# Gated recurrences: the output gate's weight tile streamed among the first scores of its own pair of heads

## What is computed

```
q, zf, zb, i, g = split(h @ w_in, 5)          # each 256 x 1024, 8 heads of 128
logf = logaddexp(log_lb, log_1m_lb + log_sigmoid(z)); k = 1 - exp(logf)   # for zf and zb
o = scan(q * 128**-0.5, k_f, logf_f, v=i) + reversed scan(q, k_b, logf_b, i)
o = rms_norm(o, g_norm) * silu(g);  y = o @ w_out
```

## Time and profile before

| | |
|---|---|
| median of 3 runs | 2884.41 us |
| the profiled execution | 2884.56 us, of which its span is 2882.7 |
| mean granted TensorE clock | 0.992 |
| busy, PE / PE weight loads / DVE / ACT / POOL | 97% / 90% / 68% / 50% / 3% |
| chain that ended last | PE 88%, DVE 6%, ACT 3% |
| this mixer, first instance | 226.31 (half 8 of pair 0) to 398.13 us (last tile) |
| this mixer, second instance | 1877.06 to 2050.07 us |

### The profile page before, as it was taken

How to read it: one execution, slowest core, us unless ns; L and a number is a source line. 1 busy time by engine, 2 the same in 40 slices (tenths; PEclk the granted TensorE clock), 3 DMA queues, 4 the chain that set the end, 5 groups by cost and what they waited for, 6 DMA issues and landing times.

```text
span 2882.7 us, 48145 instructions
## 1 busy us (share of the span) xinstructions
PE 2800.3 (97%) x20356; PEld 2594.5 (90%) x20356; DVE 1951.7 (68%) x2547; ACT 1439.9 (50%) x1970; POOL 94.5 (3%) x147
## 2 busy tenths in 40 slices
PE   9999989999998999999999999999899999999998
PEld 8999879999996999998889999998799989988997
DVE  5757876565665656556665565588755788767877
ACT  5445554444456444445644444456444644455543
POOL 0000000000012000001100000000000100000000
PEclk9999999999999999999999999999999999999999
DMA  7654436676552665663346556443465456554563
GB/s 245 205 162 147 124 120 195 190 211 184 160 171 64 202 183 175 195 187 95 108 139 185 175 191 188 154 147 111 139 194 187 151 180 207 179 161 139 175 214 102
DMA packets 406282, 478.46 MB, mean 166 GB/s; under 512 B 16634, under 2 KB 332820, under 8 KB 406068
## 3 DMA queue, kind: packets, MB, share of 16 engines
q1 hardware_dynamic: 404244, 469.07, 51.7%
q0 software_dynamic: 1632, 6.25, 0.8%
q10 hardware_dynamic: 192, 0.08, 0.0%
HBM read 474.29 MB, written 1.05 MB: 165 GB/s over the span
## 4 chain that ended last, share of the span: by engine, by line
PE 88%; DVE 6%; ACT 3%; issue 2%; POOL 0%; DMA 0%; ACTq 0%; POOLq 0%; DVEq 0%
PE Wk L710 18%; PE Wk L712 18%; PE Wk L711 18%; PE Y L710 10%; PE Y L711 10%; PE Y L712 9%; DVE w_lo L2000 2%; DVE work L2300 1%; PE Y L819 1%; PE Wk L1090 1%; ACT w_hi L1425 1%; PE Y L1000 1%; PE Y L1074 0%; PE Wk L1074 0%; PE Y L1103 0%
## 5 line engine op out<-in xcount | busy, mean ns | idle before, releaser
L2000 DVE TENSOR_TENSOR w_lo<-ring,w_hi 128x1024 fp32r<-128x1024 f32 (+2 forms) x910 | 1068.1, 1199 | 560.9 <-ACT w_hi L1425 516.9
L710 PE MATMUL Wk<-xT_hi,w_hi 128*128 128x256 f32 x4320 | 1230.0, 285 | 6.9 <-DVE w_lo L2000 3.5
L712 PE MATMUL Wk<-xT_hi,w_lo 128*128 128x256 f32 x4320 | 1222.3, 283 | 0.0
L711 PE MATMUL Wk<-xT_lo,w_hi 128*128 128x256 f32 x4320 | 1222.2, 283 | 0.0
L1425 ACT ACTIVATE w_hi<-ring 128x1024 fp32r<-128x1024 f32 (+1 forms) x894 | 906.9, 1039 | 596.9 <-PE Wk L712 420.0
L710 PEld LDWEIGHTS Wk<-xT_hi,w_hi 128*128 128x128 f32 x4320 | 828.3, 192 | 18.1 <-issue 7.0
L711 PEld LDWEIGHTS Wk<-xT_lo,w_hi 128*128 128x128 f32 x4320 | 828.5, 192 | 4.7 <-issue 1.0
L712 PEld LDWEIGHTS Wk<-xT_hi,w_lo 128*128 128x128 f32 x4320 | 828.4, 192 | 0.0
L710 PE MATMUL Y<-w_hi,hid_hi 128*128 128x512 f32 x936 | 369.1, 394 | 5.0 <-issue 3.0
L711 PE MATMUL Y<-w_lo,hid_hi 128*128 128x512 f32 x936 | 366.5, 392 | 0.0
L712 PE MATMUL Y<-w_hi,hid_lo 128*128 128x512 f32 x936 | 365.4, 390 | 0.0
(11 more groups left out here) (308 smaller groups left out, 2658.3 us busy)
## 6 DMA issues: line engine op xcount, KB each, us to landing
ring<-in_ffn_w_gu SPq DMA_DIRECT2D x352, 512.0 KB, 4.5
ring<-in_ffn_w_down SPq DMA_DIRECT2D x224, 512.0 KB, 4.2
ring<-in_ffn_w_up SPq DMA_DIRECT2D x96, 512.0 KB, 6.0
ring<-in_hg_w_in SPq DMA_DIRECT2D x80, 512.0 KB, 3.7
ring<-in_na_w_in SPq DMA_DIRECT2D x24, 512.0 KB, 4.5
ring<-in_hg_w_out SPq DMA_DIRECT2D x16, 512.0 KB, 3.3
ring<-in_lru_w_in SPq DMA_DIRECT2D x16, 512.0 KB, 4.1
ring<-in_kv_w SPq DMA_DIRECT2D x16, 512.0 KB, 5.1
```

What stands on the lines that cost most here:

```text
L710: pe.matmul(o, l_hi, r_hi, start=first, stop=False)
L711: pe.matmul(o, l_hi, r_lo, start=False, stop=False)
L712: return pe.matmul(o, l_lo, r_hi, start=False, stop=last)
L2000: ins = dve.tensor_tensor(l, r, h.bitcast(F32), ALU.subtract)
```

## The change

With `HG_LEAD = 8` the stream of halves is shifted by two against the scores. Before pair 0's score 0 only halves 4 to 7 are made. Behind scores 0 and 1 of pair p stand halves 8 and 9 (tile g) of that pair; behind scores 2 to 8 stand halves 0 to 6 of pair p+1, and then half 7. In pair 3, halves 8 and 9 stand behind scores 1 and 2, and the four `pair_out` behind scores 3 to 6; `output` and `squares_summed` of pair 2 come ahead of them. ScalarE and VectorE are shifted to match: splitting runs two units less far ahead of the scores; `save_g` moves from slot 0 to 2 (3 in the last pair), `g_sigmoid` from slot 1 to 3 (4), `gate_of` from 2 to 4 (6); `save_z` from slot 4 to 6, the sigmoid of z from slots 4, 5, 6 to 6, 7, 7; `one_minus` from 7 to 8; `save_q`, `bounded` and `start_queries` from slots 6 and 7 to 8. The clamp of the gate becomes a function of its own, `clamp_g`. Ahead of pair 0 VectorE no longer stands any split between `save_z` and `both_ways`, and `splits(base + 6)` is gone.

```diff
--- before.py
+++ after.py
@@ -29,7 +29,8 @@
 S_BANKS = (0, 1, 6)
 A_BANKS = (0, 1, 6, 7)
 MS_BANKS = (4, 4, 0, 2)
-HALVES_LAST = (0, 0, 1, 1, 2, 2, 3, 4, 5)
+HALVES_LAST = (0, 0, 1, 1, 2, 3, 3, 4, 5)
+HG_LEAD = 8
 LEVELS = 8
 SCORES = LEVELS + 1
 HALVES_AHEAD = 4
@@ -1036,22 +1037,28 @@
                     y_half(a, n, first=j == 0)
 
                 enter(s, (bank(1), bank(2)))
-                for i in range(4, 10):
+                for i in range(4, HG_LEAD):
                     half_product(0, i)
                 for p_ in range(HG_PAIRS):
                     last = p_ == HG_PAIRS - 1
                     for i in range(SCORES):
                         score(p_, i)
+                        if last and i == 0:
+                            output(p_ - 1)
+                        if last and i == 1:
+                            squares_summed(p_ - 1)
                         if not last:
-                            half_product(p_ + 1, i)
-                        if p_ and i == 2 - 2 * last:
+                            half_product(*divmod(10 * p_ + HG_LEAD + i, 10))
+                        elif 1 <= i < 3:
+                            half_product(p_, HG_LEAD + i - 1)
+                        if p_ and not last and i == 2:
                             output(p_ - 1)
-                        if p_ and i == 4 - 3 * last:
+                        if p_ and not last and i == 4:
                             squares_summed(p_ - 1)
-                        if last and i in (0, 2, 4, 6):
-                            pair_out(i // 2 % 2, i // 4)
+                        if last and 3 <= i < 7:
+                            pair_out(i % 2 == 0, (i - 3) // 2)
                     if not last:
-                        half_product(p_ + 1, 9)
+                        half_product(p_ + 1, HG_LEAD - 1)
                 output(HG_PAIRS - 1)
                 pair_out(2, 0)
                 squares_summed(HG_PAIRS - 1)
@@ -1654,7 +1661,6 @@
                 one_minus(Q0)
                 splits(base[s] + 5)
                 save_values(0)
-                splits(base[s] + 6)
                 for p_ in range(HG_PAIRS):
                     Q, last = Q0 + p_, p_ == HG_PAIRS - 1
                     for i in range(SCORES):
@@ -1664,20 +1670,22 @@
                             facing_keys(p_, i + 1)
                         if i in (0, LEVELS - 1, LEVELS):
                             keep(p_, i)
-                        if i == 1:
+                        if i == 3 + last:
                             g_sigmoid(Q)
                         if not last:
-                            ahead(HALVES_AHEAD + 10 * (p_ + 1) + i, s)
+                            ahead(HALVES_AHEAD + 10 * p_ + HG_LEAD + i, s)
                         if p_ and i == 3 and not last:
                             squares_of(p_ - 1)
                         if p_ and i == 5 - 3 * last:
                             roots(p_ - 1)
                         if not last:
-                            if 4 <= i < 7:
-                                z_sigmoid(Q + 1, i - 4)
+                            if i == 6:
+                                z_sigmoid(Q + 1, 0)
                             elif i == 7:
+                                z_sigmoid(Q + 1, 1)
+                                z_sigmoid(Q + 1, 2)
+                            elif i == LEVELS:
                                 one_minus(Q + 1)
-                            elif i == LEVELS:
                                 save_values(p_ + 1)
                         else:
                             ahead(HALVES_AHEAD + 38 + HALVES_LAST[i], s)
@@ -2244,6 +2252,10 @@
                     dve.tensor_tensor(hg_g[:, Q % 2, :].rearrange("p (a t) -> p a t", t=T),
                                       bank(4).rearrange("p (a t) -> p a t", t=T), r_wide(2), ALU.mult)\
                         .then_inc(g_saved, 1)
+
+                def clamp_g(p_):
+
+                    Q = Q0 + p_
                     dve.wait_ge(g_saved, Q + 1)
                     if Q:
                         dve.wait_ge(sg_ready, Q)
@@ -2334,26 +2346,29 @@
                 dve.wait_ge(r_ready, norms_before(s) + 1)
                 splits(base[s] + 3)
                 save_z(0)
-                splits(base[s] + 4)
+                bounded(0)
                 save_q(0)
-                bounded(0)
-                splits(base[s] + 5)
                 start_queries(0)
                 both_ways(0)
                 multiply_blocks(Q0, LEVELS - 1)
-                splits(base[s] + 6)
+                splits(base[s] + 5)
                 for p_ in range(HG_PAIRS):
                     Q, last = Q0 + p_, p_ == HG_PAIRS - 1
                     for i in range(SCORES):
+                        if last and i == 3:
+                            save_g(p_)
                         if 1 <= i < LEVELS:
                             double(p_, i)
                             if i < LEVELS - 1:
                                 keep(p_, i)
                             if 2 <= i < LEVELS - 1:
                                 multiply_blocks(Q, LEVELS - i)
-                        if i == 0:
+                        if i == 2 and not last:
                             save_g(p_)
-                        elif i == 2:
+                            clamp_g(p_)
+                        if i == 3 and last:
+                            clamp_g(p_)
+                        if i == 4 + 2 * last:
                             gate_of(p_)
                         if p_ == HG_PAIRS - 2 and i == 5:
                             split_pair(0)
@@ -2362,15 +2377,13 @@
                         if p_ and i == 6 - 3 * last:
                             normed(p_ - 1)
                         if not last:
-                            ahead(HALVES_AHEAD + 10 * (p_ + 1) + i, s)
-                            if i == 4:
+                            ahead(HALVES_AHEAD + 10 * p_ + HG_LEAD + i, s)
+                            if i == 6:
                                 save_z(p_ + 1)
-                            elif i == 6:
+                            elif i == LEVELS:
                                 save_q(p_ + 1)
-                            elif i == 7:
                                 bounded(p_ + 1)
                                 start_queries(p_ + 1)
-                            elif i == LEVELS:
                                 both_ways(p_ + 1)
                                 multiply_blocks(Q + 1, LEVELS - 1)
                         else:
```

## The result

The changed kernel takes 2901.63 us (median of three, 2901.40 to 2902.04) against 2884.41: a ratio of 1.0058 (95% interval 1.0043 to 1.0072), **17 us slower**. The direction was forecast; the size was not, for 2901.6 lies above the range's end of 2899. The profiled execution took 2902.04, of which its span is 2900.2.

What follows compares the result with a forecast made beforehand. TensorE, 88% of the chain that ended last, was taken as the bound. Instances of +2.5 and +1.4 make +3.9 at full clock; +3.2 slow outputs and +2.1 new gaps give +9.2 on 2884.4: 2893.6 us, range 2875 to 2899.

Steps and rivals of the forecast that it cites:

- start, each instance: Ahead of pair 0: halves 8 and 9 leave this stretch, so score 0 is issued 6.00 us earlier, at 226.31.
- chain from double 6 to score 0: Turn between pairs: VectorE and ScalarE steps in queue order sum to 17.7 us against TensorE's 14.2.
- pair 0: First pair's window: 42.5 us against 39.87, +2.6; in the second instance +1.5 against 40.93.
- pair 1: Second pair's window: 44.1 us against 40.48, +3.6, from waits before score 8 and the next score 0.
- pair 2: Third pair's window: about 44.8 us, +4.2, as it also splits the result of pair 0 in slot 5.
- last pair: Pair 3, from its score 0 to the last tile: 42.9 us at full clock against 44.84, -1.9.
- clock, whole kernel: TensorE clock falls: 3.2 us for slow outputs plus 2.1 for new gaps, on top of the full-clock sum.
- two slow outputs: The output of pair 3 stays as slow as before, +1.6 us in each instance, 3.2 in all.
- After a fall 0.8 of the 1.6 is hidden in pairs 1 and 2: Where VectorE waits for score 3, 0.8 us of a clock fall's 1.6 would not show; in pair 3 none is hidden.
- The first, that the clock holds: Rival: no new gap lowers the clock, +3.9 us, 2888.3; chance 0.20.
- The second (faster): Rival: pair turns are covered, decided at slot 8's low split (1.6 us); -7.9 per instance, 2869 to 2872; chance 0.18.
- The third, 2904: Rival, slower than 2899: all six gaps and the wait before pair_out drop the clock, up to +20 us; chance 0.10.

Runs made afterwards that it cites:

- the filled kernel: The changed kernel with idle products on TensorE ahead of each score 0 of pairs 1 to 3, the first pair_out and each score 8: 2887.40 us, ratio 1.0014.
- The best order found with the shift: The changed kernel with slot 8's low split, save_z, normed, one last-pair split and the gate's sigmoid in all pairs reordered: 2853.94 us, ratio 0.9901.
- the one order tried without it that gained anything: The kernel before with the gate's sigmoid behind the high split in slot 1 and normed in slot 8 ahead of the low split: 2874.20 us, ratio 0.9967.

## Why the prediction was right, and where it was wrong

| term | forecast | after, both instances | at full clock |
|---|---|---|---|
| start, each instance | -6.0 | score 0 at 226.67 (226.3 forecast), no wait | |
| chain from double 6 to score 0 | 17.7 | 17.81 (pair 1) | |
| pair 0 | 42.5 | 42.42, 42.42 | 42.43 |
| pair 1 | 44.1 | 46.59, 45.64 | 44.12 |
| pair 2 | 44.8 | 46.26, 46.25 | 44.77 |
| last pair | 42.9, or 44.5 with a slow output | 46.80, 46.98 | 42.65 |
| clock, whole kernel | 5.3 | some 15 | 0 |

**Right: the start, the chain, every pair's length, and the sign.** Score 0 of pair 0 came without a wait; the waits before score 8 were 1.36 to 2.32 (1.5 to 2.2 forecast) and before score 0 3.24, on the lines that were named. The step that carried most was to add up one chain over two queues in program order. The experiments bear out its links one by one: an early sigmoid changes nothing as long as the low split stands ahead of `bounded`; with that split moved, the wait falls from 3.24 to 0.33.

**Wrong: the clock term.** The step that failed reads "I take one per instance at about 1.05, 2.1 in all", with 3.2 for two slow outputs. From the table, pairs 1 and 2 and the last pair together are 2.47 + 1.49 + 4.15 and 1.52 + 1.48 + 4.33 over their full-clock length: 15.4 where 5.3 was forecast. The kernel at full clock closes the sum from the other side: 17.2 less 4.2 leaves 13, and of the difference to 15.4 about 1 is what came back elsewhere; the interval of the filled kernel reaches 3 to either side. Three things were mis-sized.

- How many falls. "Since the nearest pair of rows fell once in two" was the reason, and one in three turns was taken. Of the five gaps of 3.2 before a score 0, four brought the clock down. At the sixth turn, the last of the first instance, the wait of 2.32 before score 8 had brought it down first. The two halves behind that took 7.5 instead of 6.0, which left 1.76 of the wait before score 0. By then the clock was back (granted 1.00 from 357.00 to 363.00), score 0 ran in its usual 0.69, and the clock fell once more during the output behind it (0.50 from 363.75 to 366.75):

```profile
361.94 0.69 PE L1001 MATMUL Wk<-work 128*64 128x64 f32 x16 [1.76 <-DVE work L2294]
362.55 2.90 PE L1014 MATMUL Y<-work 128*128 128x256 f32 x8
```

  The prediction put the falls before score 8 and before `pair_out` at nothing. The gap of 1.87 before `pair_out` brought it down in both instances: from there to score 4 it was 4.51 and 4.18, where 2.93 is usual. The rows on which the choice rested had a gap of 1.86. The prediction itself says that the new gap is longer, and priced it all the same at a third of its turns.
- What a fall costs. "After a fall 0.8 of the 1.6 is hidden in pairs 1 and 2, where VectorE waits for score 3" runs the wrong way round: where VectorE waits for the score, whatever delays TensorE delays the whole chain. In pair 1 the slow stretch behind score 0 cost 2.44 and the pair was 2.47 longer; in the second instance it was 1.49 and 1.52. What does hide a fall is a wait of TensorE for VectorE further on: the 1.5 lost behind the 2.32 came off the wait before score 0, and pair 2 took 46.26 with that fall and 46.25 without it.
- The last pair. The term "slow as it was, +1.6" was right for its output (1.64 in the first instance), but it was not alone: 4.15 is 0.95 from the turn, 1.57 behind the gap before `pair_out`, and 1.64. In the second instance 4.33 is 1.50 behind that gap, 0.91 at score 8, and 1.9 at the output.

**The rivals.** The first, that the clock holds, was put at 2888.3; the filled kernel shows its price right (+4.2 against +3.9) and its condition not met. The second (faster) failed on the very split that it named as its deciding point; moved, it gave 2.9 a turn in waits instead of 1.6, and 22 in time, since the clock came back with it. The third, 2904, was nearest to what happened and had a chance of 0.10: at five of its six turns the clock fell, and both gaps before `pair_out` brought it down.

**Where the gain went.** The shift does what it says: 6 us per instance come out of the start and fill the gaps of pair 3. The best order found with the shift stands at -28.5, the one order tried without it that gained anything at -9.5. So shifting is worth about 19 between these two. That no order without the shift comes closer is not shown: only two were tried. In the change this gain was lost to the order inside the queues: the low split ahead of the preparation of the next pair (22), `normed` and a low split ahead of double 7 and `save_z` (12), and the gate's sigmoid ahead of a high split (7). These amounts hold their share of the clock.

What stays open: why the same gap of 3.2 left the clock alone once in five; what else the order without the shift could gain; whether the best version could go on, with TensorE's remaining waits of 1.8, 1.4, 1.2 and 0.7 in its last pair.

## What to carry to other kernels

When work is shifted between stages, write down for each in-order queue which instruction now stands ahead of the one that ends last, and sum the chain across queues: it forecast the turn to 0.1 us, and it names the one line to move. In a kernel like this one, price a gap of TensorE of 1.9 us or more as its length plus a fall of the clock of 1 to 2.5 us; one row without a fall is no evidence against it, since the same gap often falls in one instance and not in the other. Leave the fall out only where TensorE waits for another engine soon behind it. Where a gap can't be closed, a few idle products in it are worth trying.

## What was not expected of the hardware

- A gap's length alone does not say whether the clock falls. No gap up to 1.68 before a score 8 in the change did it, while one of 1.76 was followed by a fall shortly after another had ended. One of 1.87 did it both times before `pair_out`, and did not before score 6 of pair 0 in the kernel before (257.79, with 0.28 per matmul behind it). One of 2.32 did it once in two, one of 3.24 four times in five. With the experiments whose traces have the same waits unfilled, the counts are 14 of 16 for 3.24 before score 0, 6 of 8 for 2.32 before score 8 of pair 2, and 8 of 12 for 1.87 before the first `pair_out`.
- Idle products that lengthen nothing give the clock back: 7.5 us in the kernel with four gaps filled per instance, 13 with eight, while the waits themselves stay. The Trainium skill (TensorE: Matmul & The Clock Gate, HAM oscillation) has long stretches without matmuls lower the clock. The falls after single gaps of 1.87 and 2.32 go against a rule by long stretches alone, and the measurement decides.
- The clock multiplies a change of schedule. Moving one low split took 2.9 from each of six waits at most, 17.5 in all, and the time fell by 22.
